# The second expert's row list formed by one-hot products, and its gather moved up

## What is computed

```
g_idx = argmax(gl)                      # one of 4 groups for each token
top_v, top_i = top_k(el_sel, 2)         # two of the 8 experts inside that group
e = g_idx * 8 + top_i                   # 2560 (token, expert) entries over 32 experts
for each expert, its tokens in blocks of 128:
    hb = silu(xb @ w_gate[eb]) * (xb @ w_up[eb])
    yb = hb @ w_down[eb]                # weighted by the softmax of top_v, summed over a token's two entries
x = x + y;  out = rmsnorm(x)
```

## Time and profile before

| what | us |
|---|---|
| median of 3 runs | 1168.63 |
| lowest and highest run | 1165.65, 1169.90 |
| the profiled execution's own time | 1170.12 |
| span of its trace, first to last instruction | 1168.3 |

### The profile page before, as it was taken

How to read it: one execution, slowest core, us unless ns; L and a number is a source line. 1 busy time by engine, 2 the same in 40 slices (tenths; PEclk the granted TensorE clock), 3 DMA queues, 4 the chain that set the end, 5 groups by cost and what they waited for, 6 DMA issues and landing times.

```text
span 1168.3 us, 18090 instructions
## 1 busy us (share of the span) xinstructions
PE 1142.2 (98%) x5934; PEld 962.3 (82%) x5934; DVE 856.8 (73%) x1340; ACT 688.7 (59%) x1134; POOL 257.5 (22%) x348
## 2 busy tenths in 40 slices
PE   7999999999999999999999999999999999999997
PEld 7988888888889888887788888888888888888873
DVE  6649510134447766667899999999999999999966
ACT  6341241223437744334687887887877877878834
POOL 2200210001200012223242322323323323323320
PEclk9999989999999999999999999999999999999999
DMA  8212240436969644453999999999999999999998
GB/s 234 78 36 83 90 136 1 128 141 207 316 236 370 227 145 145 149 195 139 408 379 388 394 384 406 382 398 393 380 396 387 384 396 388 393 398 388 386 266 348
DMA packets 110146, 324.09 MB, mean 277 GB/s; under 512 B 22454, under 2 KB 59232, under 8 KB 85520
## 3 DMA queue, kind: packets, MB, share of 16 engines
q1 hardware_dynamic: 92384, 279.17, 64.4%
q0 software_dynamic: 17712, 44.27, 10.5%
HBM read 285.37 MB, written 51.12 MB: 288 GB/s over the span
## 4 chain that ended last, share of the span: by engine, by line
PE 89%; DMA 6%; DVE 2%; ACT 1%; issue 1%; SPq 0%; POOL 0%; POOLq 0%; DVEq 0%; ACTq 0%
PE psum L935 26%; PE psum L937 26%; PE psum L936 25%; PE psum L1219 2%; DMA units<-mlstm_units 2%; PE psum L1253 1%; PE psum L1125 1%; PE psum L1297 1%; PE psum L1060 1%; DMA w_row<-entry_weights,first_row 1%; PE psum L1061 1%; PE psum L1106 1%; PE psum L981 1%; DMA e_st<-expert_rows 1%; PE psum L949 1%
## 5 line engine op out<-in xcount | busy, mean ns | idle before, releaser
L2035 DVE TENSOR_TENSOR e_lo<-e_st,e_hi 128x1024 fp32r<-128x1024 f32 x384 | 444.5, 1219 | 10.8 <-ACT e_hi L1531 10.7
L1531 ACT ACTIVATE e_hi<-e_st 128x1024 fp32r<-128x1024 f32 x384 | 375.8, 1052 | 9.7 <-DMA e_st<-in_expert_w_gate_dram 4.6
L937 PE MATMUL psum<-e_hi,ex_lo 128*128 128x512 f32 x512 | 199.4, 390 | 0.0
L935 PE MATMUL psum<-e_hi,ex_hi 128*128 128x512 f32 x512 | 199.4, 389 | 0.1
L936 PE MATMUL psum<-e_lo,ex_hi 128*128 128x512 f32 x512 | 199.2, 389 | 0.0
L935 PE MATMUL psum<-xT_hi,w_hi 128*128 128x512 f32 (+1 forms) x432 | 151.5, 351 | 2.2 <-DVE w_lo L1671 1.4
L936 PE MATMUL psum<-xT_lo,w_hi 128*128 128x512 f32 (+1 forms) x432 | 149.6, 346 | 0.0
L937 PE MATMUL psum<-xT_hi,w_lo 128*128 128x512 f32 (+1 forms) x432 | 149.5, 346 | 0.0
L935 PEld LDWEIGHTS psum<-e_hi,ex_hi 128*128 128x128 f32 x512 | 96.1, 188 | 20.5 <-DVE ex_lo L2106 0.5
L937 PEld LDWEIGHTS psum<-e_hi,ex_lo 128*128 128x128 f32 x512 | 96.1, 188 | 20.0
L936 PEld LDWEIGHTS psum<-e_lo,ex_hi 128*128 128x128 f32 x512 | 96.1, 188 | 19.9
(11 more groups left out here) (292 smaller groups left out, 1858.9 us busy)
## 6 DMA issues: line engine op xcount, KB each, us to landing
e_st<-in_expert_w_gate_dram SPq DMA_DIRECT2D x64, 1024.0 KB, 8.0
e_st<-in_expert_w_up_dram SPq DMA_DIRECT2D x64, 1024.0 KB, 9.4
e_st<-in_expert_w_down_dram SPq DMA_DIRECT2D x64, 1024.0 KB, 10.9
mlstm_units<-stage SPq DMA_DIRECT2D x18, 640.0 KB, 3.7
w_st<-in_w_in_dram SPq DMA_DIRECT2D x20, 512.0 KB, 4.4
xn_scratch<-xn POOLq DMA_DIRECT2D x20, 512.0 KB, 3.9
stage<-gate_rows SPq DMA_DIRECT2D x18, 512.0 KB, 5.8
e_st<-expert_rows SPq DMA_DIRECT2D x15, 512.0 KB, 8.8
```

The lines of the kernel that those rows point to most:

```text
L935: pe.matmul(out, a_hi, b_hi, start=start, stop=False)
L937: return pe.matmul(out, a_lo, b_hi, start=False, stop=stop)
L1531: act.activation(e_hi[:, r, :, :], e_st[:, slot, :, :], ACT.Copy).then_inc(ehi_done, 1)
L2035: dve.tensor_tensor(e_lo[:, r, :, :], e_st[:, slot, :, :], e_hi[:, r, :, :].bitcast(F32), ALU.subtract).then_inc(elo_done, 1)
```

## The change

VectorE makes a second one-hot matrix for each tile, for the expert that step 1 serves (`expert_at(1)`, column 8 of `rank` and `chosen`; its places are counted from 1, so 1 is taken off first). TensorE multiplies it by the same token numbers into another PSUM bank, VectorE reads that product too, and `first_row` has two columns. On GpSimd `rows_in(1, 1)` now stands directly behind `rows_in(0, 0)`, before the last `entries_out`; the two `weights_in` no longer have the wait for `first_rows` ahead of them. The counts of the semaphores `slots_done`, `totals_ready` and `totals_read` follow. The two one-hot tiles take the space of the one before, since bf16 tiles are now allotted two bytes an element.

```
-    first_row = const("first_row", [P, 1], I32)
+    first_row = const("first_row", [P, 2], I32)
...
-    one_hot_rows = cbuf("one_hot_rows", [P, NT, P], BF16)
+    one_hots = cbuf("one_hots", [P, 2, NT, P], BF16)
+    one_hot_rows = [one_hots[:, e, :, :] for e in range(2)]
...
             def rows_in(i, b):
...
-                    rows = rows_to[:, i:i + 1] if i else first_row[:, :]
+                    rows = rows_to[:, i:i + 1] if i > 1 else first_row[:, i:i + 1]
...
             rows_in(0, 0)
             pool.sem_inc(pool_step, 1)
+            pool.wait_ge(totals_read, 2)
+            rows_in(1, 1)
             entries_out(NT - 1)
             pool.wait_ge(weights_step, 3)
             pool.dma_start(w_dram.rearrange("(q p) a -> q (p a)", p=P), w_rows[:, :]).then_inc(table_set, 16)
             pool.wait_ge(table_set, 32)
-            pool.wait_ge(first_rows, 16)
-            rows_in(1, 1)
             weights_in(0, 0)
             weights_in(1, 1)
+            pool.wait_ge(first_rows, 16)
...
-            pe.wait_ge(slots_done, 2 * NT - 1)
-            for t in range(NT):
-                last = pe.matmul(psum[:, 7, 200:202], one_hot_rows[:, t, :], token_parts[:, t, :], start=(t == 0),
-                                 stop=(t == NT - 1))
-            last.then_inc(totals_ready, 1)
+            for e in range(2):
+                pe.wait_ge(slots_done, 3 * NT - 2 + e)
+                for t in range(NT):
+                    last = pe.matmul(psum[:, 7 - e, 200:202], one_hot_rows[e][:, t, :], token_parts[:, t, :],
+                                     start=(t == 0), stop=(t == NT - 1))
+                last.then_inc(totals_ready, 1)
...
             def list_rank(t):
...
+                second = expert_at(1)
+                link(dve.tensor_scalar(rt[:, 333:334], rank[:, second:second + 1], -1.0, None, ALU.add))
+                dve.scalar_tensor_tensor(out=one_hot_rows[1][:, t, :], in0=slot_ramp[:, :], scalar=rt[:, 333:334],
+                                         in1=chosen[:, t, second:second + 1].broadcast_to([P, P]), op0=ALU.is_equal,
+                                         op1=ALU.mult).then_inc(slots_done, 1)
...
-            dve.wait_ge(totals_ready, 1)
-            link(dve.tensor_reduce(rt[:, 330:331], psum[:, 7, 200:202], AX.X, ALU.add))
-            dve.tensor_scalar(first_row[:, :], rt[:, 330:331], 2.0 * T, None, ALU.add).then_inc(totals_read, 1)
+            for e in range(2):
+                dve.wait_ge(totals_ready, e + 1)
+                link(dve.tensor_reduce(rt[:, 330 + 2 * e:331 + 2 * e], psum[:, 7 - e, 200:202], AX.X, ALU.add))
+                dve.tensor_scalar(first_row[:, e:e + 1], rt[:, 330 + 2 * e:331 + 2 * e], 2.0 * T, None,
+                                  ALU.add).then_inc(totals_read, 1)
             list_slots(i)
```

More of the change, by code:

```diff
@@ L187, in cbuf @@
         off = c_off[0]
-        c_off[0] += (int(np.prod(shape[1:])) * 4 + 31) // 32 * 32
+        c_off[0] += (int(np.prod(shape[1:])) * (2 if dt == BF16 else 4) + 31) // 32 * 32
         return at(name, off, shape, dt)
@@ L492, in load_half_steps @@
         def load_half_steps(eng):
-            eng.wait_ge(totals_read, 2)
+            eng.wait_ge(totals_read, 3)
             return eng.value_load(half_steps[0:1, 0:1], min_val=0, max_val=E // 2 * (NT - 1)) + E // 2
@@ L817, in entries_out @@
             def entries_out(i):
-                pool.wait_ge(slots_done, 2 * i + 2)
+                pool.wait_ge(slots_done, 3 * i + 3)
                 for k in range(2):
@@ L1120, in router @@
                     pe.wait_ge(logits_taken, t)
-                    pe.wait_ge(slots_done, 2 * t)
+                    pe.wait_ge(slots_done, 3 * t)
                 else:
@@ L1138, in ranks @@
                 pe.wait_ge(chosen_done, t + 1)
-                wait(pe, slots_done, 2 * t)
+                wait(pe, slots_done, 3 * t)
                 for t2 in range(t):
@@ L2012, in list_rank @@
                 dve.wait_ge(rank_ready, t + 1)
-                wait(dve, slots_done, 2 * t)
+                wait(dve, slots_done, 3 * t)
                 link(dve.scalar_tensor_tensor(out=rank, in0=psum[:, 7, 64:64 + E], scalar=float(E), in1=ebase[:, :],
                                               op0=ALU.mult, op1=ALU.add))
-                dve.scalar_tensor_tensor(out=one_hot_rows[:, t, :], in0=slot_ramp[:, :], scalar=rank[:, 0:1],
+                dve.scalar_tensor_tensor(out=one_hot_rows[0][:, t, :], in0=slot_ramp[:, :], scalar=rank[:, 0:1],
                                          in1=chosen[:, t, 0:1].broadcast_to([P, P]), op0=ALU.is_equal,
+                                         op1=ALU.mult).then_inc(slots_done, 1)
[3 more added lines that the diff above has]
+                                         in1=chosen[:, t, second:second + 1].broadcast_to([P, P]), op0=ALU.is_equal,
                                          op1=ALU.mult).then_inc(slots_done, 1)
@@ L2087, in _ @@
             list_rank(i)
-            dve.wait_ge(totals_ready, 1)
-            link(dve.tensor_reduce(rt[:, 330:331], psum[:, 7, 200:202], AX.X, ALU.add))
-            dve.tensor_scalar(first_row[:, :], rt[:, 330:331], 2.0 * T, None, ALU.add).then_inc(totals_read, 1)
+            for e in range(2):
[3 more added lines that the diff above has]
+                                  ALU.add).then_inc(totals_read, 1)
             list_slots(i)
-            dve.wait_ge(totals_ready, 2)
+            dve.wait_ge(totals_ready, 3)
             link(dve.tensor_reduce(rt[0:1, 331:332], psum[0:1, 5, 0:E], AX.X, ALU.max))
```

## The result

| kernel | median, us | lowest to highest | runs | ratio to before, 95% interval |
|---|---|---|---|---|
| before | 1166.97 | 1164.50 to 1169.98 | 18 | |
| changed | 1170.84 | 1167.54 to 1173.86 | 18 | 1.0027 [1.0017, 1.0038] |

What follows compares the result with a forecast made beforehand. Two late transfers, step 1's gather and step 0's factors, were taken to bound the second `gate_up`. Of 2.32 us to be had, VectorE's added work takes 0.73, leaving 1.59: 1168.63 - 1.59 = 1167.0 us, range 1164.8 to 1169.5.

Steps and rivals of the forecast that it cites:

- What bounds the kernel: At the second `gate_up`: two late transfers, step 1's gather and step 0's factors, set its start; gains read at 569.78.
- My 564: On GpSimd's queue: the factors of step 0 land at 564 us, within 563.1 to 566.6, before `hh` wants them at 566.74.
- VectorE's cost: On VectorE: added one-hot work delays the first gather by 0.27 us and the first `gate_up` by 0.73 us.
- GpSimd's queue: List writes and factors behind the early gather stay in time; with writes of 1.94 us each, factors land by 568 at worst.
- SP's queue: Step 1's weight loads, behind SP's wait for the lists, issue 1.6 us later, with some 10 us of cover; cost nothing.
- Slower, the factors late: Rival: GpSimd's chain of gather, list writes and factors lands at 569.2, costing 0.9 us: 1169.5; chance 0.05.
- the order in a ring: GpSimd's DMA queue: list writes and factors' write cannot pass the second gather's rows; at 9 us they land behind 557.1.
- The factors stay last: Rival: at `hh`, factors land behind 566.74 and TensorE still waits for them; gain 0.3 to 0.8 us, 1167.8; chance 0.12.
- hidden additions: Rival: VectorE's added work is hidden ahead of the first `gate_up`, keeping the whole 2.32 us: 1166.3; chance 0.07.
- nothing: Rival: the second gather comes as late as before, and VectorE's work costs 0.7 us: 1169.4; chance 0.04.
- The clock: Rival: TensorE's clock falls to 1.2 GHz for the first `gate_up`, whose 11 us become 22: 1178; chance 0.02.

Runs made afterwards that it cites:

- e9: Changed kernel with VectorE's first `e_lo` held until both writes of the last list entries had landed; run once, 1173.31 us, no ratio.
- e6: Changed kernel with two loads (four pieces) of step 1's weights issued ahead of SP's wait for the lists; ratio to before 0.9998.
- e2: Changed kernel with the second gather behind the last two list writes instead of ahead of them; ratio to before 1.0021.
- e11: The same kernel as e6, run again; ratio to before 0.9991.
- e7: Changed kernel with step 1's row numbers all out of range, so its gather and factors' read move nothing; run once, no ratio.
- e3: Changed kernel with the second gather and both reads of the factors back behind the wait for `first_rows`; ratio to before 1.0000.
- e10: Kernel before, with only the read of step 0's factors moved ahead of the wait for `first_rows`; ratio to before 0.9992.
- e5: Changed kernel with the second gather directly behind the factors' write on GpSimd; ratio to before 0.9997.
- e12: Changed kernel with the second gather behind both reads of the factors, still ahead of the wait for `first_rows`; ratio to before 1.0005.
- e8: Changed kernel with GpSimd's semaphore raise moved behind both list writes, meant to hold back VectorE's first `e_lo`; run once, no ratio.

## Why the prediction was wrong

**What bounds the kernel: right in its place.** The gain was to be read at the second `gate_up`, and there the loss sits. Both transfers that were late before came in time: no wait for the second `gx`, and the factors landed 6.5 to 6.8 us behind 556.64, at about 563.3, while `sg` ended at 566.6. My 564 on the old scale is 17.3 us behind the first gather, and they landed 18.6 behind it.

**VectorE's cost: about right in size.** From the last turn of `x` to the logits of tile 9 it is 537.69 - 534.77 = 2.92 against 2.62, so 0.30 (0.27 said). The first gather is issued 9.90 behind against 9.32, so 0.58 later (0.27 said), and the reading of the lists' places starts 9.23 behind against 8.33, 0.90 later (0.73 said). The first `gate_up` starts 17.70 behind against 17.01, so 0.69 (0.73 said); in the other traces with the added one-hots, e9 left out, it is 17.73 to 18.09, so up to 1.08. It is no longer released by `ex_lo`, as was forecast, but follows the filler without a wait.

**GpSimd's queue: a term mis-sized.** "If both took the 1.94 of the factors' read" was meant as the worst for the list writes. It was taken from the longest row in sight rather than from what made that row long. The write of 1.42 us in the earlier trace rows had ended at the first of two fixed points of VectorE's work, L + 2.07, and the change made the next one end at the second, L + 5.69, which took 3.27 us. I had named the mechanism and its page, and then priced it by the rows that it had touched lightly; the 1.94 us of the factors' read is itself one of them, made at 559.26 beside the `e_lo` pair of 557.96. The last write ended 8.0 us behind the first gather; my worst case was 6.9.

**SP's queue: the step that failed.** Of these loads the prediction says "They have some 10 us before the second `gate_up`" and "I cost both at nothing". But they are needed for `hh`, well ahead of the second `gate_up`: ScalarE and VectorE take their lists in order, and the `e_hi` and `e_lo` of step 1's first four pieces stand ahead of `sg` and `hh`. In the trace of before the last of these `e_lo` pairs begins at 563.31 and takes 2.36, so it ends at 565.67, and `hh` was forecast for 566.74. The cover was 1.1 us, not 10. The loads came 5.3 us later behind the first gather, not 1.6 (11.07 against 5.73 for the list read), and the last `e_lo` 3.7 us later (567.58 - 544.67 = 22.91 against 565.67 - 546.48 = 19.19). Even the forecast 1.6 us would have eaten 0.5 of the gain: 565.67 + 1.6 = 567.27 against 566.74. e6 shows the link: with those two loads alone moved, `hh` is free of `e_lo` and the start comes 2.9 us sooner.

**The rivals.** *Slower, the factors late* had the right sign and the wrong queue, but e2 and e11 show that the mechanism is real. Its price, a landing at 569.2, follows from none of its rows: with the second gather slowed to 9 us, the writes land behind 557.1, and 557.1 + 0.3 + 9.0 = 566.4 was still in time for 566.74. That the early gather's transfer would hold the writes up by the order in a ring isn't borne out either: in e7 it moves nothing, and the list read is as late (10.93 against 11.07). *The factors stay last*, *hidden additions* and *nothing* didn't come: `w_row` wasn't late, the first `gate_up` moved, and the second gather was early. *The clock* was given 0.02 and priced for a wait ahead of the first `gate_up`, at 1178. The fall that cost time came ahead of the second one, where the late `hh` made one hole of 3.71 us. The forecast idle time of 1.6 us before the turn of the factors didn't come: with the clock at 0.50 the filler in front of it took longer, and nothing was lost. I had read "the clock stood at 1.00" in the earlier trace rows as safety; but there the old kernel's wait was cut in two by the turn of the second `gx`. The very success of the early gather took that turn out of the middle of the wait. In e3, where the wait of 2.84 us is still in front of the turn, the clock stays at 1.00. The Trainium skill, "TensorE: Matmul & The Clock Gate", section "What's actually happening", has an idle TensorE fall to half its clock; the trace agrees, with 0.50 from about 567.8 to 571.2 us.

**The account.** 1.7 to 2.4 us for the late start and 1.0 to 1.4 for the clock give 2.7 and 3.8 us in the two traces of the changed kernel; the timings say 3.2 and 1.8, so stage and timing agree in size and no closer. Of the forecast gain of 1.6 us, e10 and e6 show 1.1 and 1.2 us at the start of the second `gate_up`, in one trace each, and e6's kernel run again was 1.8 us later than the kernel before. No ordering that was tried makes a gain that this timing can tell from none.

## What to carry to other kernels

Ask of every load that a change delays for whom it is *first* needed in the in-order list of the engine that prepares it, not when its product is used: here 1.1 us of cover was read as 10. An indirect DMA of GpSimd beside back-to-back VectorE work on two SBUF tiles is priced by where it falls in that work, not by the row of one that ran alone. And when one of two waits at a place is removed, look whether the remaining ones join into a hole that costs TensorE its clock.

## What the runs showed of the hardware that I had not expected

- Indirect DMAs on GpSimd beside back-to-back `e_lo` ended at fixed points of VectorE's work: 2.1 us behind its start in all traces but e9's, and 5.7 us behind it in ten, whichever DMA it was and whether it moved data or not (3.27 us against 1.0 alone). One under way when `e_lo` began wasn't held, nor was the factors' write, a plain DMA (0.59 or 0.60 us throughout).
- A write of 10 KB took 1.7 us to land ahead of the weight loads (before), 3.2 in the changed kernel, 5.4 and 5.6 when they were issued ahead of it (e11, e6), and 8.1 with a gather also just ahead (e2).
- The clock fell behind a hole of 2.23 us (e5) and not behind one of 2.84 us that a turn of a `gx` followed (e3), nor behind one of 1.87 us (e12). In e2 and e8, behind holes of 3.95 and 4.57 us, it stayed at 0.50 for some 7 us instead of 3.4, and the second `gate_up` lost 2.3 and 2.1 us.
- A semaphore raised in GpSimd's list didn't wait for the indirect DMAs ahead of it to be made: it was up by 548.46 us, and the second of them began at 550.88 (e8).
